# Differential attention: a unit's first steps moved in front of the logits in the first and in the last head

## The chip, the core and the metric

One core of a Trainium2 chip runs the whole program. The time is that of the device in microseconds (us), from the start to the end of one execution; the runs of the kernel before have a median of 1680.06 us (three runs, 1678.5 to 1680.33).

## What is computed

The reference is one step of a backbone with two layers: a gated linear attention layer and a differential attention layer, each followed by a SwiGLU FFN, over 512 sample tokens and 128 prompt tokens, width 1024, all in float32. The change touches the differential attention only. Cut to what matters (q and k of the sample tokens are rotated by `apply_rope` first; the prompt tokens attend among themselves; the 512 sample tokens attend to 256 old keys and to each other):

```python
q, k, v = diff_qkv(h, w_qkv)                     # 8 heads; q, k: 2 maps of 64; v: 128
s = jnp.einsum('bqhcd,bkhcd->bhcqk', qi, k) * (DIFF_DH ** -0.5)
p = jax.nn.softmax(s, axis=-1)
w = p[:, :, 0] - lam * p[:, :, 1]
o = jnp.einsum('bhqk,bkhv->bqhv', w, v)
o = rmsnorm(o, g_head) * (1.0 - lam_init)
x = x + gate * (o.reshape(B, T, 1024) @ w_out)
```

## The kernel before, in words

Every engine has its own instruction stream, written out by hand, and they meet at semaphores only. TensorE takes its matmuls in the order of the text.

**Units.** A unit is the product of a 1024x128 block of weights with the normed activations of all 640 tokens: 8 steps, one for each 128 rows of the weights, of 6 matmuls each (`tile_products`, L826). Float32 precision comes from three products: high weights by high activations, high by low, low by high. So each block is loaded into `w_raw` (SyncE, `load`, L578), its high part is made by ScalarE (`split_hi`, L1522) and its low part by VectorE (`split_lo`, L2280). There are two weight buffers; units take them in turn (slot 0, slot 1). A head has three units, for q, k and v (j = 0, 1, 2); behind the last head the same places are filled by the output projection's units, which have six or seven steps at first (`out_steps`, L1334). All these units but one sum in the same accumulator, `acc[0]`, so the first step of a unit waits until VectorE has read the unit before (`unit_scaled`, L3030, for a head's units; `out_add`, L3178, which adds an output unit to x in three instructions).

**Logits.** For each head there are four tiles of 128 queries, with two maps each, and the prompt's own tile. `logits` (L1399) writes the two maps of a tile into two of three rotating buffers in PSUM (work, side and the second accumulator `acc[1]`), whose order is the list `RING` (L472): tile 0 takes two, the prompt's tile the third, and tile 1 takes the two of tile 0 again. `begin` (L1298) waits until the buffer has been read by its last user. That user is ScalarE's exponential (`exps`, L2092), which itself waits for VectorE's maximum (`maxima`, L3108). VectorE then combines the two maps (`combine`), TensorE turns the result (`w_turn`), ScalarE copies it and TensorE multiplies it with the values.

**Periods.** All engines go through periods p = -1 to 8. In period p TensorE does head p's logits and turns, and between them the steps of head p+1's units, so that each waits for the other as little as may be. The text of TensorE's period is at L1457, ScalarE's at L2184, VectorE's at L3188. In period 8 and in the units behind period 7 the output projection takes the place of the next head. In period 0 head 0's v unit is the last thing before the first logits: VectorE reads its result (`unit_scaled(0, 2)`) behind the low parts of the old and new keys (`past_lo`, `k_lo_part`), the copy of the new key (`k_keep`) and the split of the next unit's weights (`unit_lo(1, 0)`). SyncE's queue carries in turn the rotation copies of q and k (`rotation`, L697) and the loads of the next head's weights (`head_load`, L677; `out_load`, L683); GpSimd's queue carries the old keys and values, and the new ones out.

The wait that the first step of head 1's first unit makes (slot 1, so the last branch):

```python
                    if h == 0:
                        pe.wait_ge(acc_free[0], pair)
                    elif slot == 0:
                        pe.wait_ge(acc_free[1], pair)
                    else:
                        pe.wait_ge(acc_free[0], pair + 1)
```

Of the kernel before, what the change touches and what calls it, by code (L numbers as in the profile page):

```python
# [37 lines left out]
AH, DH = 8, 64  # L38
# [35 lines left out]
def program(nc, x_prompt, x_sample, state_f, state_b, cache_k, cache_v, c, c_ctx, w_ada, b_ada, g_mix, g_ffn,  # L74
# [3 lines left out]
    with ctx:  # L78
# [443 lines left out]
        def live(h):  # L522
            return 0 <= h < AH
# [301 lines left out]
        def _(pe):  # L825
# [485 lines left out]
            def unit_steps(h, j, a, b):  # L1311

                if h >= AH:
                    out_steps(3 * (h - AH) + j, a, b)
                    return
                if not live(h) or (h == 0 and j < 2):
                    return
                pair, slot = head_unit(h, j)
                if a == 0:
                    pe.wait_ge(lo_ready, unit(pair, slot) + 1)  # L1320
# [6 lines that stand above are left out]
                for k in range(a, b):  # L1327
                    mm = tile_products(slot, k, KD, h_hi_k, h_lo_k, acc[0], 2)
                    if k == KD - 1:
                        mm.then_inc(unit_mm, 1)  # L1330
                    elif (h, j) == (AH - 1, 2):
                        mm.then_inc(h_read, 1)
# [66 lines left out]
            def logits(h, q):  # L1399
                if not live(h):  # L1400
                    return
                names = [f"S{q}{m}" for m in range(2)]
                outs = [begin(h, name) for name in names]
                if q == 0:
                    operands_ready(h)
                for a, b in ((0, 512), (512, SK)):
                    map_products(h, [out[:, a:b] for out in outs], slice(q * P, (q + 1) * P), slice(a, b),
                                 names if b == SK else None)
# [20 lines left out]
            def values(h, pp):  # L1429
                if not live(h):  # L1430
                    return
                out = begin(h, f"O{pp}")
                for q in (2 * pp, 2 * pp + 1):
                    pe.wait_ge(buf_free[buf_of(h, f"T{q}")], count_of(h, f"T{q}") + 1)
                if pp == 0:
                    pe.wait_ge(vp_in[h % 2], 16 * (h // 2 + 1))
                    pe.wait_ge(buf_free[buf_of(h, "VT")], count_of(h, "VT") + 1)
                for t in range(SK // P):
                    mm = pe.matmul(out[:, 0:2 * P], vv[h % 2][:, t, :], wt[pp][:, t, :],  # L1439
                                   start=(t == 0), stop=(t == SK // P - 1))  # L1440
                if pp:
                    mm = pe.matmul(out[:, 512:512 + P], vv[h % 2][:, KT - 1, :], wtp[:, :], start=True, stop=True)
                mm.then_inc(buf_mm[buf_of(h, f"O{pp}")], 1)
# [13 lines left out]
            def period(p):  # L1457

                values(p - 1, 1)
                logits(p, 0)  # L1460
                prompt_logits(p)
                unit_steps(p + 1, 0, 0, 4)
                o_squares_sum(p - 1)
                logits(p, 1)
                unit_steps(p + 1, 0, 4, 6)
                v_turn(p)
                unit_steps(p + 1, 0, 6, 8)
                logits(p, 2)
                unit_steps(p + 1, 1, 0, 2)
                w_turn(p, 0)  # L1470
                unit_steps(p + 1, 1, 2, 8)
                logits(p, 3)
                unit_steps(p + 1, 2, 0, 2)
                if p < 0:
                    k_turn(0)
                w_turn(p, 1)
                unit_steps(p + 1, 2, 2, 5)
                w_turn(p, 2)
                unit_steps(p + 1, 2, 5, 8)
                w_turn(p, 3)  # L1480
                if p >= 0:
                    k_turn(p + 1)
                values(p, 0)
# [37 lines left out]
        def _(act):  # L1521
# [603 lines left out]
            def w_read(h, q):  # L2125
                if not live(h):
                    return
                out = done(h, f"T{q}")
                op = act.activation(wt[q // 2][:, :, (q % 2) * P:(q % 2 + 1) * P],
                                    out[:, 0:SK].rearrange("p (t n) -> p t n", n=P), ACT.Copy)  # L2130
                if q:
                    free(op, h, f"T{q}")
# [51 lines left out]
            def period(p):  # L2184

                past_hi(p)
                w_read(p - 1, 3)
                k_hi_part(p)
                if p == 0:
                    unit_hi(1, 0)  # L2190
                    unit_read(0, 2)
                o_read(p - 1, 0)
                last_o_hi(p, KD - 2)
                unit_hi(p + 1, 1)
                last_o_hi(p, 2, 3)
                o_read(p - 1, 1)
                o_square(p - 1)
                exps(p, 0, 0)
                exps(p, 0, 1)
                prompt_exps(p)  # L2200
                scaled(p, 0)
                last_o_hi(p, 4, 5)
                o_log(p - 1)
                exps(p, 1, 1)
                exps(p, 1, 0)
                scaled(p, 4)
                unit_read(p + 1, 0)
                v_copy(p)
                o_exp(p - 1)
                unit_hi(p + 1, 2)  # L2210
                last_o_hi(p, KD - 1)
                w_read(p, 0)
                exps(p, 2, 1)
                exps(p, 2, 0)
                scaled(p, 1)
                unit_read(p + 1, 1)
                prompt_w_read(p)
                scaled(p, 2)
                exps(p, 3, 1)
                exps(p, 3, 0)  # L2220
                scaled(p, 3)
                w_read(p, 1)
                w_read(p, 2)
                q_hi_part(p + 1)
                if p >= 0:
                    unit_hi(p + 2, 0)
                    last_o_hi(p, 0, 1)
                    unit_read(p + 1, 2)
# [50 lines left out]
        def _(dve):  # L2279
# [908 lines left out]
            def period(p):  # L3188

                past_lo(p)  # L3190
                k_lo_part(p)
                k_keep(p)
                unit_lo(p + 1, 0)
                if p == 0:
                    unit_scaled(0, 2)
                last_o_lo(p, 2, 3, KD - 2)
                if p == AH:
                    for name in ("T13", "T2", "T4"):
                        weight_sum(1, 0, name)
                maxima(p, 0, 0)  # L3200
                maxima(p, 0, 1)
                o_square_lo(p - 1)
                prompt_maxima(p)
                norms(p, 0)
                last_o_lo(p, 4, 5)
                o_variance(p - 1)
                maxima(p, 1, 1)
                maxima(p, 1, 0)
                norms(p, 4)
                combine(p, 0)  # L3210
                unit_lo(p + 1, 1)
                if p >= 0:
                    unit_scaled(p + 1, 0)
                combine(p, 4)
                norms(p, 1)
                out_add(p, 0)
                maxima(p, 2, 0)
                maxima(p, 2, 1)
                out_add(p, 3)
                o_newton(p - 1)  # L3220
                if p == AH:
                    o_scale(p - 1)
                unit_lo(p + 1, 2)
                out_add(p, 4)
                last_o_lo(p, KD - 1)
                if p == AH:
                    split_lo(*out_unit(6), OUT_KT[6])
                out_add(p, 5)
                norms(p, 2)
                combine(p, 1)  # L3230
                unit_scaled(p + 1, 1)
                out_add(p, 1)
                maxima(p, 3, 1)
                maxima(p, 3, 0)
                combine(p, 2)
                rope_sin(p + 1, 0)
                rope_cos(p + 1, 0)
                norms(p, 3)
                rope_add(p + 1, 0)
                rope_cos(p + 1, 1)  # L3240
                combine(p, 3)
                rope_sin(p + 1, 1)
                if p < AH:
                    o_scale(p - 1)
                q_lo_part(p + 1)
                rope_add(p + 1, 1)
                out_add(p, 2)
                if p >= 0:
                    unit_scaled(p + 1, 2)
                last_o_lo(p, 0, 1)  # L3250
# [106 lines left out]
```

## Time and profile before

| | |
|---|---|
| median of 3 runs | 1680.06 us |
| profiled execution, in all | 1682.3 us |
| its span | 1680.5 us |
| TensorE busy (matmuls) | 1621.0 us, 96% |
| VectorE, ScalarE, GpSimd busy | 1174.0, 845.0, 97.4 us |
| chain that ended last | TensorE 92%, VectorE 3%, ScalarE 2% |
| granted TensorE clock, mean | 0.985 |

The profile is one execution; its span is what the engines' records cover, and the time in all is a little longer. The attention periods lie at about 865 to 1163 us of the span, some 37 us for each head. A row of the time order has the start, the duration, the engine, the line of the kernel, the operation, what is written from what, and how many such instructions stand together; in brackets, the idle time of the engine before it and the instruction that ended it. Durations overlap a little, since the next instruction starts before the last one is written back. The granted clock is a share of full speed.

### The profile page before, as it was taken

The numbers are of one execution on the slowest core, as the hardware profiler recorded it, in microseconds if no ns is written. First come the engines' busy times: TensorE is split into PE (matmuls) and PEld (weight loads), VectorE is DVE, ScalarE is ACT, GpSimd is POOL, SyncE is SP. The second block draws the span as 40 slices with busy tenths as digits, with TensorE's granted clock in tenths as the row PEclk, the third lists the DMA queues.
The fourth block names the chain that finished last, engine by engine and source line by source line (L and its number), as shares of the span: only waits on it lengthen the run. The fifth ranks groups of instructions, "written<-read, shape, count | busy, mean of one in ns | idle before, by whom it ended". The sixth has DMA issues, their size and how long they took to land.

```text
span 1680.5 us, 28352 instructions
## 1 busy us (share of the span) xinstructions
PE 1621.0 (96%) x10988; PEld 1521.9 (91%) x10988; DVE 1174.0 (70%) x2033; ACT 845.0 (50%) x1460; POOL 97.4 (6%) x147
## 2 busy tenths in 40 slices
PE   6999999998999999999999999999889999999997
PEld 4878788798999999999989999998879999999997
DVE  5536455678857858767767887787878588586775
ACT  4534525356524515334547777786655244253444
POOL 1111110200000000000000000000000000000000
PEclk9999999999999999999999999999989999999998
DMA  9544453632333323432322222213122232232312
GB/s 319 167 154 138 134 186 107 198 85 76 120 107 101 120 70 88 122 92 91 100 72 75 65 74 63 78 45 120 56 76 70 79 88 80 67 97 64 101 40 87
DMA packets 230393, 171.06 MB, mean 102 GB/s; under 512 B 10643, under 2 KB 210998, under 8 KB 230262
## 3 DMA queue, kind: packets, MB, share of 16 engines
q1 hardware_dynamic: 216182, 120.37, 24.8%
q0 software_dynamic: 14080, 48.90, 8.5%
q8 instruction: 88, 1.44, 0.3%
q14 instruction: 43, 0.35, 0.1%
HBM read 160.32 MB, written 4.72 MB: 98 GB/s over the span
## 4 chain that ended last, share of the span: by engine, by line
PE 92%; DVE 3%; ACT 2%; issue 1%; DMA 1%; SPq 0%; POOL 0%; DVEq 0%; ACTq 0%; POOLq 0%
PE acc L832 44%; PE acc L1215 28%; PE side L1215 4%; PE side L1394 2%; PE side L1439 1%; PE acc L1439 1%; PE side L867 1%; PE work L1368 1%; DVE x L2658 1%; PE work L867 1%; PE side L1054 1%; PE acc L1036 0%; PE acc L867 0%; PE work L1394 0%; PE acc L1088 0%
## 5 line engine op out<-in xcount | busy, mean ns | idle before, releaser
L832 PE MATMUL acc<-h_hi,w_hi 128*128 128x320 f32 x1006 | 243.9, 324 | 8.5 <-DVE w_lo L2283 2.5
L832 PE MATMUL acc<-h_lo,w_hi 128*128 128x320 f32 x1006 | 231.8, 312 | 0.0
L832 PE MATMUL acc<-h_hi,w_lo 128*128 128x320 f32 x1006 | 230.8, 311 | 0.0
L832 PEld LDWEIGHTS acc<-h_hi,w_hi 128*128 128x128 f32 x1006 | 166.3, 191 | 35.7 <-issue 21.0
L2658 DVE SCALAR_TENSOR_TENSOR x<-acc,mods,x 128x320 f32<-128x320 f32 (+2 forms) x249 | 94.1, 434 | 135.2 <-PE acc L832 135.1
L1215 PE MATMUL acc<-h_hi,w_hi 128*128 128x322 f32 x616 | 169.9, 317 | 13.6 <-ACT u_t L1924 13.6
L832 PEld LDWEIGHTS acc<-h_lo,w_hi 128*128 128x128 f32 x1006 | 170.9, 191 | 0.0
L832 PEld LDWEIGHTS acc<-h_hi,w_lo 128*128 128x128 f32 x1006 | 170.8, 190 | 0.0
L1215 PE MATMUL acc<-ax_hi,ff_hi 128*128 128x322 f32 x528 | 166.9, 316 | 3.5 <-issue 3.5
L1215 PE MATMUL acc<-ax_lo,ff_hi 128*128 128x322 f32 x528 | 165.5, 313 | 0.0
L1215 PE MATMUL acc<-ax_hi,ff_lo 128*128 128x322 f32 x528 | 165.5, 313 | 0.0
L832 PE MATMUL acc<-hid_hi,ff_hi 128*128 128x320 f32 x616 | 140.7, 310 | 0.0
L832 PE MATMUL acc<-hid_lo,ff_hi 128*128 128x320 f32 x616 | 140.3, 309 | 0.0
L832 PE MATMUL acc<-hid_hi,ff_lo 128*128 128x320 f32 x616 | 140.3, 309 | 0.0
L1215 PE MATMUL acc<-h_lo,w_hi 128*128 128x322 f32 x440 | 138.7, 315 | 0.0
L2283 DVE TENSOR_TENSOR w_lo<-w_raw,w_hi 128x1024 fp32r<-128x1024 f32 (+2 forms) x66 | 78.4, 1189 | 74.0 <-ACT w_hi L1527 73.8
L1215 PEld LDWEIGHTS acc<-h_hi,w_hi 128*128 128x128 f32 x616 | 112.8, 193 | 14.6 <-issue 14.0
L1215 PE MATMUL acc<-h_hi,w_lo 128*128 128x322 f32 x440 | 121.2, 310 | 0.0
L1215 PEld LDWEIGHTS acc<-ax_hi,ff_hi 128*128 128x128 f32 x528 | 101.3, 192 | 8.1 <-issue 7.9
L832 PEld LDWEIGHTS acc<-hid_lo,ff_hi 128*128 128x128 f32 x616 | 103.0, 188 | 0.0
L832 PEld LDWEIGHTS acc<-hid_hi,ff_lo 128*128 128x128 f32 x616 | 103.0, 188 | 0.0
L832 PEld LDWEIGHTS acc<-hid_hi,ff_hi 128*128 128x128 f32 x616 | 102.8, 188 | 0.0
(461 smaller groups left out, 3569.8 us busy)
## 6 DMA issues: line engine op xcount, KB each, us to landing
a_raw<-in_w_ada_dram POOLq DMA_DIRECT2D x80, 512.0 KB, 6.0
ff_raw<-in_w_ffn_gate_dram SPq DMA_DIRECT2D x88, 256.0 KB, 3.3
ff_raw<-in_w_ffn_up_dram SPq DMA_DIRECT2D x88, 256.0 KB, 4.3
w_raw<-in_w_gla_in_dram SPq DMA_DIRECT2D x24, 512.0 KB, 3.8
ff_raw<-in_w_ffn_down_dram SPq DMA_DIRECT2D x32, 384.0 KB, 3.4
w_raw<-in_w_diff_qkv_dram SPq DMA_DIRECT2D x24, 512.0 KB, 3.9
ff_raw<-in_w_ffn_down_dram SPq DMA_DIRECT2D x32, 320.0 KB, 3.2
a_left<-in_w_ada_dram SPq DMA_DIRECT2D x8, 512.0 KB, 9.7
```

The lines of the kernel that those rows point to most:

```text
L832: mm = pe.matmul(out[:, s, 0:HALF + s * more], w[:, k * P:(k + 1) * P], a(k)[:, s * HALF:(s + 1) * HALF + s * more], start=(k == 0 and n = ...
L867: mm = pe.matmul(out[q * CG:(q + 1) * CG, 0:512], cond_at(2 * q + j, place), a_raw[q][:, j, :], start=(b == lo and j == 0), stop=(b == hi ...
L1054: mm = pe.matmul(out[cc * CH:(cc + 1) * CH, r], q_d[d][:, t * P + cc * CH:t * P + (cc + 1) * CH], state_in(d, 2 * t + cc), start=False, st ...
L1215: mm = pe.matmul(out, w[:, j * P:(j + 1) * P], x_part, start=(name in ("P1", "P7", "P2") and j == 0 and n == 0), stop=(j == JT - 1 and n = ...
L1368: mm = pe.transpose(out[:, t * P:(t + 1) * P], tile, ident[:, :])
L1394: mm = pe.matmul(outs[m], qq[h % 2][rows, cols], kk[h % 2][rows, keys], start=(n == 0), stop=(n == 2))
L1439: mm = pe.matmul(out[:, 0:2 * P], vv[h % 2][:, t, :], wt[pp][:, t, :], start=(t == 0), stop=(t == SK // P - 1))
L2283: dve.tensor_tensor(w_lo[slot][:, 0:kt * P], w_raw[slot][:, 0:kt * P], w_hi[slot][:, 0:kt * P].bitcast(F32), ALU.subtract).then_inc(lo_rea ...
L2658: op = dve.scalar_tensor_tensor(out=xk[:, lo:hi], in0=src[:, half, lo - half * HALF:hi - half * HALF], scalar=mods[:, one, v], in1=xk[:, l ...
```

## The change

Nothing is computed differently; instructions change places.

In the first head (p = 0) TensorE does the first four steps of head 1's first unit before the logits of tile 0 instead of behind them and the prompt's. Its weights' high part is made by ScalarE before the new key's high part instead of after it, and its low part by VectorE in the period before (p = -1), between the cosine product of the key and `combine` (which does nothing there). In the last head (p = 7) TensorE does the first three steps of the second output unit before the logits of tile 2 instead of two steps behind them. VectorE makes that unit's low weights before `o_variance`, and adds the first output unit to x (`out_add(p, 0)`) between the two maxima of tile 1 instead of behind the norms of tile 1; `out_add(p, 0)` does something in period 7 only.

```diff
@@ TensorE's period
                 values(p - 1, 1)
+                if p == 0:
+                    unit_steps(1, 0, 0, 4)
                 logits(p, 0)
                 prompt_logits(p)
-                unit_steps(p + 1, 0, 0, 4)
+                if p:
+                    unit_steps(p + 1, 0, 0, 4)
                 o_squares_sum(p - 1)
                 logits(p, 1)
                 unit_steps(p + 1, 0, 4, 6)
                 v_turn(p)
                 unit_steps(p + 1, 0, 6, 8)
+                if p == AH - 1:
+                    unit_steps(p + 1, 1, 0, 3)
                 logits(p, 2)
-                unit_steps(p + 1, 1, 0, 2)
+                if p != AH - 1:
+                    unit_steps(p + 1, 1, 0, 2)
                 w_turn(p, 0)
-                unit_steps(p + 1, 1, 2, 8)
+                unit_steps(p + 1, 1, 3 if p == AH - 1 else 2, 8)
@@ ScalarE's period
                 w_read(p - 1, 3)
+                if p == 0:
+                    unit_hi(1, 0)
                 k_hi_part(p)
                 if p == 0:
-                    unit_hi(1, 0)
                     unit_read(0, 2)
@@ VectorE's period
                 k_keep(p)
-                unit_lo(p + 1, 0)
+                if p:
+                    unit_lo(p + 1, 0)
                 if p == 0:
                     unit_scaled(0, 2)
...
                 last_o_lo(p, 4, 5)
+                if p == AH - 1:
+                    unit_lo(p + 1, 1)
                 o_variance(p - 1)
                 maxima(p, 1, 1)
+                out_add(p, 0)
                 maxima(p, 1, 0)
                 norms(p, 4)
                 combine(p, 0)
-                unit_lo(p + 1, 1)
+                if p != AH - 1:
+                    unit_lo(p + 1, 1)
...
                 norms(p, 1)
-                out_add(p, 0)
...
                 rope_cos(p + 1, 1)
+                if p == -1:
+                    unit_lo(1, 0)
                 combine(p, 3)
```

## Rows read from the trace of the kernel before

**Rows 1.** The page, its first part: busy time and share of the span of each engine.

```profile
PE 1621.0 (96%) x10988; PEld 1521.9 (91%) x10988; DVE 1174.0 (70%) x2033; ACT 845.0 (50%) x1460; POOL 97.4 (6%) x147
```

**Rows 2.** TensorE's waits, whole span: who ended them, us, times, longest.

```profile
PE side L1394 <- ACT w_map L2103: 2.9, 1, 2.9
```

**Rows 3.** Time order of TensorE, first head: logits, four steps, logits of tile 1.

```profile
864.82 0.47 PE L1394 MATMUL side<-kk_hi,q_hi 64*128 64x512 f32 x1 [2.50 <-DVE kk_lo L3089]
...
866.86 0.87 PE L832 MATMUL acc<-h_hi,w_hi 128*128 128x320 f32 x2 [0.42 <-DVE v_f L3047]
...
871.85 0.50 PE L1394 MATMUL side<-kk_hi,q_hi 64*128 64x512 f32 x1
```

**Rows 4.** Time order of VectorE, first head: rotated key, split, read of v.

```profile
860.90 0.69 DVE L3069 TENSOR_TENSOR rotated<-rotated,sin_t 128x512 f32<-128x512 f32 x1 [3.02 <-DMA rotated<-k_f]
...
864.68 1.23 DVE L2283 TENSOR_TENSOR w_lo<-w_raw,w_hi 128x1024 fp32r<-128x1024 f32 x1
...
865.89 0.82 DVE L3047 TENSOR_TENSOR v_f<-acc,rstd_a 128x640 f32<-128x640 f32 x1
```

**Rows 5.** First head: ScalarE's idle time, the weights' load, such loads' time to landing.

```profile
862.97 0.74 ACT L2090 ACTIVATE kk_hi<-k_f 128x640 fp32r<-128x640 f32 x1 [4.64 <-DVE k_f L3075]
...
853.53 0.58 SPq L578 DMA_DIRECT2D w_raw<-in_w_diff_qkv_dram  x1
...
w_raw<-in_w_diff_qkv_dram SPq DMA_DIRECT2D x3, 512.0 KB, 4.0
```

**Rows 6.** Last head, tile 0: logits (TensorE), first maximum (VectorE), last exponential's sum (ScalarE).

```profile
1125.44 0.49 PE L1394 MATMUL side<-kk_hi,q_hi 64*128 64x512 f32 x1
...
1126.80 0.96 DVE L3112 TENSOR_REDUCE stat<-work 128x1 f32<-128x768 f32 x1 [0.46 <-PE work L1394]
...
1129.47 0.19 ACT L2103 ACTIVATION_READ_ACCUMULATOR p<-side,stat 128x1 f32 x1
```

**Rows 7.** Stretches of TensorE: length, busy time (instructions), granted clock, DMA share, GB/s.

```profile
866.86:869.67 2.81, 2.81 (x10) 0.50 0.79 231
1139.46:1146.29 6.83, 6.22 (x28) 0.51 0.99 304
1126.97:1130.60 3.63, 3.63 (x27) 1.00 0.24 71
```

**Rows 8.** The same, around stalls of 1.59 us (to 337.38) and 2.21 us (to 1193.11).

```profile
335.79:340.80 5.01, 3.42 (x23) 1.00 0.71 204
1190.90:1197.40 6.50, 4.29 (x19) 0.74 0.00 0
```

**Rows 9.** Time order of TensorE, last head: tile 2's logits, two steps, turn, third unit.

```profile
1138.32 0.50 PE L1394 MATMUL side<-kk_hi,q_hi 64*128 64x512 f32 x1 [2.87 <-ACT w_map L2103]
...
1140.36 0.87 PE L832 MATMUL acc<-h_hi,w_hi 128*128 128x320 f32 x2 [0.61 <-issue]
...
1143.70 1.49 PE L1368 MATMUL work<-ident,w_map 128*128 128x128 f32 x6
...
1151.04 0.54 PE L832 MATMUL acc<-h_hi,w_hi 128*128 128x320 f32 x2 [0.48 <-issue]
```

**Rows 10.** Time order of VectorE, last head: from the variance to the second unit's x update.

```profile
1133.49 0.82 DVE L3153 TENSOR_SCALAR o_var<-work 128x640 f32<-128x640 f32 x1
...
1140.18 0.95 DVE L3112 TENSOR_REDUCE stat<-side 128x1 f32<-128x768 f32 x1
...
1144.36 0.95 DVE L2283 TENSOR_TENSOR w_lo<-w_raw,w_hi 128x768 fp32r<-128x768 f32 x1
1148.04 0.17 DVE L3127 RECIPROCAL stat<-stat 128x2 f32<-128x2 f32 x1 [2.74 <-ACT w_map L2103]
...
1148.87 1.02 DVE L3140 SCALAR_TENSOR_TENSOR w_map<-p,stat,w_map 128x768 f32<-128x768 f32 x1 [0.47 <-ACT w_map L2123]
1149.81 1.13 DVE L2658 SCALAR_TENSOR_TENSOR x<-acc,mods,x 128x320 f32<-128x320 f32 x3
```

**Rows 11.** Time order of ScalarE, last head: the copy of tile 0's turned weights.

```profile
1145.43 0.81 ACT L2129 ACTIVATE wt<-work 128x768 f32<-128x768 f32 x1 [4.93 <-PE work L1368]
```

## The prediction, made before the changed kernel ran

> **What bounds the kernel now.** I read the page first, then TensorE's waits, then the time order of TensorE, VectorE and ScalarE around the two edited places. TensorE is busy for 96% of the 1680.5 us [rows 1], so only what it waits for, and the clock it is granted, can give time. Its longest wait in the attention stage is 2.9 us for an exponential, in the last head [rows 2]; in front of the first head's logits it waits 2.50 us for the low part of the new keys. With the short waits beside them (0.42, 0.61 and 0.48 us [rows 3, 9]) they are 6.9 us: nothing here can bring much more than that and the low clock behind it.
>
> In the first head TensorE ends v's unit at 862.32 (864.82 less 2.50), runs the logits of tile 0 and of the prompt until 866.44 (866.86 less 0.42), and then waits for VectorE's read of v's accumulator. Four steps of head 1's first unit start at 866.86, the logits of tile 1 follow at 871.85 without a wait [rows 3]. In the last head it ends the transposes of v at 1135.45 (1138.32 less 2.87), the logits of tile 2 at 1139.75, and starts the second output unit at 1140.36 and the third at 1151.04 [rows 9].
>
> **The clock.** TensorE has half clock, the lower of 1.2 and 2.4 GHz, in 866.86 to 869.67, after 2.50 us of idling, and in 1139.46 to 1146.29, after 2.87 and 0.61 us [rows 7]. Four steps take 3.63 us at full clock [rows 7] and 4.99 in the first head with the low stretch in them (866.86 to 871.85 [rows 3]): such a stretch costs 1.4 us. Two steps wholly at low clock take 3.34 us (1140.36 to 1143.70 [rows 9]), so four take 6.7. Elsewhere a stall of 1.59 us left the granted clock at full, and one that ended at 1193.11 after 2.21 us was followed by low clock [rows 8]. Between those two lengths I can only bound.
>
> **First head.** The four steps (24 matmuls, 24 weight loads) move ahead of 18 logits matmuls, and their weights must be split earlier. That is easy: the load was issued at 853.53 and such loads land after 4.0 us, about 857.6, while ScalarE idles 4.64 us until 862.97 and VectorE 3.02 us until 860.90 [rows 4, 5]. Two splits, each at most the 1.23 us of VectorE's row [rows 4], end by 860.7 even if ScalarE begins at 858.3, just ahead of VectorE's turn at 860.90. I cost them at nothing; a load 0.5 us later would delay the key's chain by 0.3. SyncE's next load into that buffer waits for this split and goes out 5 us earlier; its weights are wanted in the middle of the head, so that gains nothing. GpSimd's queue is not touched.
>
> But the steps write the accumulator that holds v's result, so they wait until VectorE has read it, and that read stays behind the key's low part and the copy of the new key. It ends now at 865.89 + 0.82 = 866.71. Without the split in front (1.23 us, 1.15 by the distance of the starts) it ends at 865.56, and TensorE starts the steps 0.15 later, as now: **865.71**. The idle of 2.50 us before the logits becomes one of 3.39 before the steps. The logits' operands are ready at 864.8, but TensorE takes its matmuls in order. With one low stretch as now the steps take 4.99 us: logits of tile 0 at **870.70** instead of 864.82.
>
> Next late are the logits of tile 1. They write the two buffers of tile 0's logits, which come free with tile 0's two exponentials. Where that runs undisturbed, in the last head, the logits start at 1125.44, the first maximum at 1126.80, and the last exponential's sum is read by 1129.66 [rows 6]: 4.22 us, 4.27 to the next matmul. Today the four steps cover this. After the change only the prompt's logits stand there (1.62 us with tile 0's, 864.82 to 866.44), so TensorE stalls 2.65 us and starts tile 1 at 870.70 + 4.27 = **874.97**, against 871.85: **3.1 us later**. From there to the last head TensorE has no wait, so it reaches the end in full. Bounds: steps at full clock (3.63) give +1.8, wholly at low clock (6.7) +4.8. The second stall, longer than the 2.21 us that was followed by low clock, brings a second low stretch: +1.4, with ends 0 and 1.6. First head: **+4.5**, from +1.8 to +6.4.
>
> **Last head.** Three steps of the second output unit go ahead of tile 2's logits. They need its low weights, and the first output unit read from the accumulator; both are moved up. VectorE's variance started at 1133.49; the split (0.95) now stands before it, so variance, first maximum of tile 1 and x update follow at about 1134.4, 1135.1 and 1135.95 (the first output unit is done before v's transposes, in time). The update takes 1.13 us [rows 10]: 1137.1. The steps start at **1137.2**: 1.75 us of idling instead of 2.87. The second maximum is late by 1.9 us and its exponential ends at about 1139.0 (0.95 for each by half of the 1.90 between 1127.76 and 1129.66 [rows 6]); the logarithm, 0.9 later through the variance, is in time for that. The steps' 2.7 us (three quarters of 3.63) last until 1139.9 and cover it.
>
> Logits of tile 2 then run 1139.95 to 1141.4, against 1139.75 now. What decides the third unit's start is VectorE's chain behind them: two maxima and three Newton instructions (1140.18 to 1144.36), a split (0.95), the norms, the combination (1.02), and the x update of the second unit (1.13) [rows 10]. Today it stands still from 1145.3 to 1148.04, because ScalarE waits for TensorE's turn of tile 0 until 1145.43 [rows 11]. After the change that turn runs at 1141.4 and the chain is unbroken: 1141.35 + 4.18 + 0.95 + 0.2 + 1.02 + 1.13 = 1148.8 (0.2 estimated for the two small norms from the 0.17 of one). Third unit at **1148.9** instead of 1151.04: **-2.1 us**, with a new stall of 2.5 us before it, as TensorE ends tile 3's logits at 1146.4. Output units 3 and 4 are loaded from 1134.4 and 1146.4 on and wanted ten us later: hidden. Clock: the 1.75 us stall is nearer the 1.59 that cost nothing; the 2.5 us one is of the kind that does: +1.4, ends 0 and +2.8. Last head: **-0.7**, from -2.1 to +0.7.
>
> **Sum:** 4.5 - 0.7 = +3.8 us. The profiled execution took 1682.3 us, 2.2 over the median of the three runs, 1680.06; the difference is applied to the median: 1683.9, rounded to **1684.0**.
>
> **A rule on the clock.** The Trainium skill, "TensorE: Matmul & The Clock Gate" (Terms), puts the penalty of throttled time at half of it. By that the stretch of 6.83 us cost 3.4, of which 0.6 was idle anyway, and each 2.8 us stretch 1.4, as the rows have it: the sum by the rule is the same within 0.3. Its section "HAM oscillation" speaks against the change: a kernel that stalls between bursts is throttled again at each burst. The trace agrees for stalls from 2.21 us up, not for the one of 1.59 [rows 8].
>
> **Rivals.** (1) *Every stall costs a low stretch*, that of 1.75 us too, and the low clock lasts through the first steps: +1.4 or +1.7, together 1685.3 to 1687. For it: the low stretch of the last head lasts 6.83 us though only 3.5 were idle [rows 7, 9]. Against: the stall of 1.59. Chance 0.18; this is the case of the skill's rule on bursts. (2) *The clock holds* behind the second stall of the first head and the 2.5 us stall of the last: 1683.9 - 2.8 = 1681.1, or 1679.8 with the first steps at full clock. For it: a fall depends on the moment of the stall as well; against: 2.21 us was enough. Chance 0.24. (3) *Faster: the accumulator is free early.* Could the steps start behind v's unit at 862.5, they would end at 866.1 at full clock, tile 1 would start at 870.4, 1.5 us earlier, and with the last head's -2.1 the time is 1676.5. It decides as soon as v's read ends before about 863. Against: today's 0.42 us wait is on that very read [rows 3], and its place behind the key stays. Chance 0.08.
>
> **How the numbers follow.** The forecast has 0.50. A measurement of this kernel can tell 0.2%, 3.4 us, from no change, so the border, 1683.4, lies inside the forecast's own spread (1682.4 to 1685.6): I give it 0.35 slower and 0.15 same. With rival 1 slower is 0.53, with rival 2 same is 0.39, and rival 3 is faster, 0.08. The range, 1679.8 to 1687.5, takes in rivals 1 and 2 and leaves out rival 3 and chains of ends.
>
> **What would show it.** In the changed profile: one wait of TensorE of about 3.4 us on v_f ahead of the first steps, none on kk_lo, and one of about 2.6 us on an exponential before tile 1's logits, with low clock behind both. In the last head a wait of 1.75 us on the x update before the steps, none before tile 2's logits, and 2.5 us on the x update before the third unit. I am wrong if tile 1's logits in the first head start without a wait, or if VectorE reads v before the key's low part.

## The result and the profile after

The changed kernel takes 1686.24 us (median of 7 runs, 1683.34 to 1687.58) against 1679.52 us for the kernel before (7 runs, 1678.02 to 1680.87). The ratio is 1.0035, with a 95% interval of 1.0024 to 1.0045: by it the change costs 5.9 us (4.0 to 7.6); the two medians alone differ by 6.7. The prediction was 1684.0, 3.8 us slower, with a range of 1679.8 to 1687.5: the measured time is in the range, but above the spread that the forecast itself had (1682.4 to 1685.6).

TensorE's three longest entries in the list of its waits in the attention stage of the changed kernel (who waited for whom, us in total, times, longest) answer to [rows 2, 3, 9]:

```profile
PE acc L832 <- issue: 3.5, 2, 2.4
PE acc L832 <- DVE v_f L3054: 3.3, 1, 3.3
PE side L1394 <- ACT p L2109: 2.8, 1, 2.8
```

The two long waits of before, on the low part of the keys and on the exponential in the last head, are gone. Three others of 3.3, 2.8 and 2.4 us stand in their place. "issue" means that no record names who ended the wait; the time order of VectorE below lets one infer it.

The first head in TensorE's time order of the changed kernel: the first of the four steps, then the logits of tiles 0, 1 and 2.

```profile
865.68 0.53 PE L832 MATMUL acc<-h_hi,w_hi 128*128 128x320 f32 x2 [3.33 <-DVE v_f L3054]
...
870.92 0.50 PE L1394 MATMUL side<-kk_hi,q_hi 64*128 64x512 f32 x1
...
875.29 0.47 PE L1394 MATMUL side<-kk_hi,q_hi 64*128 64x512 f32 x1 [2.75 <-ACT p L2109]
...
882.37 0.50 PE L1394 MATMUL side<-kk_hi,q_hi 64*128 64x512 f32 x1
```

VectorE there: the read of v's result, then idle for 6.74 us until tile 0's logits are there.

```profile
863.71 0.82 DVE L3096 TENSOR_TENSOR kk_lo<-k_f,kk_hi 128x640 fp32r<-128x640 f32 x1 [0.47 <-ACT kk_hi L2096]
864.46 0.28 DVE L3113 COPY k_new<-work 128x128 f32<-128x128 f32 x1
...
864.72 0.81 DVE L3054 TENSOR_TENSOR v_f<-acc,rstd_a 128x640 f32<-128x640 f32 x1
872.28 0.96 DVE L3119 TENSOR_REDUCE stat<-side 128x1 f32<-128x768 f32 x1 [6.74 <-PE side L1394]
```

Stretches of TensorE in the changed kernel (length, busy time, granted clock, DMA share, GB/s): the four steps, from tile 1's logits to tile 2's, and the third output unit's first steps.

```profile
865.68:870.92 5.24, 5.24 (x24) 0.67 0.11 38
875.29:882.37 7.08, 7.08 (x42) 0.76 0.00 1
1153.81:1157.01 3.20, 3.20 (x13) 0.53 0.51 145
```

The reader should see three starts. The steps start at 865.68, the predicted 865.71. Tile 1's logits start at 875.29 (predicted 874.97) instead of 871.85 [rows 3], 3.4 us later. From there to tile 2's logits is 7.08 us, where it was 5.52 us; the difference of 1.56 us goes with the second low stretch (granted clock 0.76).

The last head in TensorE's time order of the changed kernel: the transposes of v, the second unit's first steps, the logits of tiles 2 and 3, the third unit.

```profile
1140.26 0.74 PE L1368 MATMUL work<-ident,v_f 128*128 128x128 f32 x5 [0.42 <-DVE o_var L3160]
...
1142.12 0.53 PE L832 MATMUL acc<-h_hi,w_hi 128*128 128x320 f32 x2 [1.12 <-issue]
...
1144.94 0.50 PE L1394 MATMUL side<-kk_hi,q_hi 64*128 64x512 f32 x1
...
1150.09 0.49 PE L1394 MATMUL side<-kk_hi,q_hi 64*128 64x512 f32 x1 [0.28 <-ACT w_map L2109]
...
1153.81 0.87 PE L832 MATMUL acc<-h_hi,w_hi 128*128 128x320 f32 x2 [2.42 <-issue]
```

VectorE in front of the second unit's steps: the x update of the first output unit, which ends at 1142.01, just before the steps start at 1142.12.

```profile
1140.89 1.12 DVE L2665 SCALAR_TENSOR_TENSOR x<-acc,mods,x 128x320 f32<-128x320 f32 x3
```

And VectorE behind tile 2's logits: the chain from the first maximum over the Newton step to the x update that frees the accumulator, unbroken (each row's start is the end of the one before, less the overlap). It ends at 1153.71, and the third unit starts at 1153.81. It answers to [rows 10], where VectorE stood still until 1148.04.

```profile
1146.30 0.96 DVE L3119 TENSOR_REDUCE stat<-side 128x1 f32<-128x768 f32 x1 [1.29 <-PE side L1394]
1147.18 0.95 DVE L3119 TENSOR_REDUCE stat<-acc 128x1 f32<-128x768 f32 x1
1148.04 0.81 DVE L2318 SCALAR_TENSOR_TENSOR o_sqr<-o_inv 128x640 f32<-128x640 f32 x1
1148.89 0.83 DVE L2321 TENSOR_TENSOR o_sqr<-o_sqr,o_var 128x640 f32<-128x640 f32 x1
1149.75 0.82 DVE L2323 SCALAR_TENSOR_TENSOR o_inv<-o_sqr,o_inv 128x640 f32<-128x640 f32 x1
1150.49 0.95 DVE L2290 TENSOR_TENSOR w_lo<-w_raw,w_hi 128x768 fp32r<-128x768 f32 x1
1151.36 0.16 DVE L3134 RECIPROCAL stat<-stat 128x2 f32<-128x2 f32 x1
1151.56 0.16 DVE L3138 TENSOR_TENSOR stat<-stat,lam_neg 128x1 f32<-128x1 f32 x1
1151.64 1.02 DVE L3147 SCALAR_TENSOR_TENSOR w_map<-p,stat,w_map 128x768 f32<-128x768 f32 x1
1152.58 1.13 DVE L2665 SCALAR_TENSOR_TENSOR x<-acc,mods,x 128x320 f32<-128x320 f32 x3
```

### The profile page after: what moved, and what is told of

Read it like the earlier page. It is cut to its first block, busy times and chain, and to the rows that moved or that the text cites. A ratio compares the mean times of both kernels' runs of the same rounds, so it can differ in the third digit from the quotient of the medians.

```text
span 1684.4 us, 28352 instructions
## 1 busy us (share of the span) xinstructions
PE 1620.9 (96%) x10988; PEld 1522.5 (90%) x10988; DVE 1174.0 (70%) x2033; ACT 845.3 (50%) x1460; POOL 97.4 (6%) x147
## 4 chain that ended last, share of the span: by engine, by line
PE 92%; DVE 4%; ACT 2%; issue 1%; DMA 0%; SPq 0%; POOL 0%; DVEq 0%; ACTq 0%; POOLq 0%
PE acc L832 44%; PE acc L1215 28%; PE side L1215 4%; PE side L1394 2%; PE side L1439 1%; PE acc L1439 1%; PE side L867 1%; PE work L1368 1%; DVE x L2665 1%; PE work L867 1%; PE side L1054 1%; PE acc L1036 0%; PE work L1394 0%; PE acc L867 0%; PE acc L1088 0%
```

## The experiments

Each was timed beside the kernel before; gains and losses in us are the ratio's distance from 1 times 1680, and an interval of 0.001 each way is 1.7 us. The table gives the ratios and two distances in each one's profile, worked out from the starts in TensorE's time order. "First head" is from the first head's key transposes to tile 0's logits of the last head; "last head" from those logits to the third output unit's first matmul. The first distance takes in six more heads, which no edit touches. Each distance is from one execution, so differences of some tenths of a us between rows mean little.

| kernel | ratio to before (95%) | first head, us | last head, us |
|---|---|---|---|
| before, first profile | 1 | 268.98 | 25.60 |
| before, profiled again (before_again) | 1.0000 (0.9991 to 1.0009) | 268.95 | 23.95 |
| the change | 1.0035 (1.0024 to 1.0045) | 273.90 | 23.43 |
| first head's part only (first_only) | 1.0030 (1.0020 to 1.0039) | 273.83 | 25.33 |
| last head's part only (last_only) | 1.0004 (0.9996 to 1.0013) | 269.26 | 23.41 |
| steps spread (cover) | 1.0007 (0.9998 to 1.0016) | 270.84 | 24.84 |
| v read first (vread) | 1.0008 (0.9999 to 1.0017) | 270.75 | 24.88 |
| both of these (both) | 0.9994 (0.9985 to 1.0003) | 267.41 | 25.43 |
| early split only (split_only) | 0.9999 (0.9990 to 1.0008) | 269.42 | 25.59 |
| late Newton step (late_newton) | 0.9976 (0.9966 to 0.9986) | 269.25 | 20.94 |
| late Newton step, no steps moved (newton_only) | 0.9995 (0.9986 to 1.0004) | 269.23 | 23.36 |
| both, with late Newton step (best) | 0.9977 (0.9967 to 0.9987) | 269.17 | 20.92 |
| late Newton step and early split (best2) | 0.9977 (0.9968 to 0.9986) | 268.95 | 20.90 |

### The kernel before, profiled again

No edit.

> The kernel before, unchanged, profiled once more and timed. It serves to see what of the first profile was chance. The first profiled execution took 1682.3 us, 2.2 over the median, and had 6.83 us of low clock in the last head. Theory (the clock's fall depends on the moment as well): this profile has the same waits (2.50 and 0.42 us in the first head, 2.87, 0.61 and 0.48 us in the last) within 0.1 us, but stretches of low clock of another length, and its time differs by about 0.45 us for each us of low clock. Rival (the stretches belong to the kernel): the same stretches within 0.5 us.

Measured: ratio 1.0000, this profile at 1679.53 us in all, 2.8 under the first. TensorE's waits in its attention stage:

```profile
PE side L1394 <- ACT w_map L2103: 2.9, 1, 2.9
PE side L1394 <- DVE kk_lo L3089: 2.8, 1, 2.8
PE acc L832 <- issue: 0.9, 1, 0.9
```

The low clock comes at another moment here: the logits behind the long wait run slow from the start (0.79 us a row where the first profile has 0.50 [rows 9]).

```profile
1136.96 0.79 PE L1394 MATMUL side<-kk_hi,q_hi 64*128 64x512 f32 x1 [2.85 <-ACT w_map L2103]
```

The stretch 1130 to 1165, first in the first profile of before, then in this one:

```profile
1130.00:1165.00 35.00, 30.76 (x195) 0.90 0.42 132
```

```profile
1130.00:1165.00 35.00, 30.97 (x205) 0.95 0.41 132
```

The long waits are much alike (2.76 and 2.85 instead of 2.50 and 2.87), the short ones are not: those of 0.42 and 0.61 us are absent, as the slower logits in front of them fill that time, and the last is 0.87 instead of 0.48. So the theory's "within 0.1 us" is missed, and a wait of some tenths says as much of the clock as of the kernel. The low clock differs: 35 us at 0.90 are about 7 us at half clock, at 0.95 half as many, and the third output unit comes 1.65 us earlier (23.95 instead of 25.60). That is not the whole of the 2.8 us between the two executions. Another 1.3 us lies ahead of the attention, where the change does nothing: the first head's key transposes start at 856.46 in the first profile and at 855.13 in this one.

```profile
856.46 0.44 PE L1368 MATMUL work<-ident,k_past 128*128 128x128 f32 x2 [0.28 <-ACT k_f L2061]
```

```profile
855.13 0.44 PE L1368 MATMUL work<-ident,k_past 128*128 128x128 f32 x2 [0.27 <-ACT k_f L2061]
```

So the profile on which I predicted had bad luck in the place where I saw a gain. In the seven kernels and profiles with the last head's order of before on both engines, the distance lies anywhere from 23.95 to 25.60.

### The two halves of the change

The first head's part alone is the change with this taken back:

```diff
-                if p == AH - 1:
-                    unit_steps(p + 1, 1, 0, 3)
                 logits(p, 2)
-                if p != AH - 1:
-                    unit_steps(p + 1, 1, 0, 2)
+                unit_steps(p + 1, 1, 0, 2)
...
-                if p == AH - 1:
-                    unit_lo(p + 1, 1)
                 o_variance(p - 1)
                 maxima(p, 1, 1)
-                out_add(p, 0)
```

The last head's part alone is the change with this taken back:

```diff
-                if p == 0:
-                    unit_steps(1, 0, 0, 4)
                 logits(p, 0)
                 prompt_logits(p)
-                if p:
-                    unit_steps(p + 1, 0, 0, 4)
+                unit_steps(p + 1, 0, 0, 4)
...
-                if p == -1:
-                    unit_lo(1, 0)
```

and in both cases with the other lines that belong to that head.

> Only the first head's part of the change. Theory (v's read in front, cover lost behind): TensorE waits 3.3 us on v_f before the first steps and 2.7 us on the exponential before tile 1's logits; tile 1's logits are 3.4 us later than before, tile 2's 5.0 us with a second low stretch, 3.4 if the clock holds; the ratio to before 1.0020 to 1.0035. Rival (the two heads share the loss): ratio below 1.0015.

> Only the last head's part of the change. Theory: the third output unit starts 2.1 us earlier than before with a wait of 2.4 us in front of it; the time is 0.5 to 2 us shorter, ratio 0.9985 to 1.0000. Rival (the last head's part costs too, by the split in front of the variance and the x update between the maxima): 1 us or more longer, ratio over 1.0006.

Measured: 1.0030 for the first head's part, 1.0004 for the last head's. In the first, TensorE waits 3.36 us on v_f and 2.76 on the exponential, tile 1's logits stand 18.81 us behind the key transposes (before: 15.39, so 3.4 later) and tile 2's 25.85 (20.91, 4.9 later): as expected. The rival, a loss shared between the heads, is out: the first head alone has nearly all of it. In the second, the third unit has its wait of 2.41 us and comes after 23.41 us, 2.2 earlier than in the first profile of before but only 0.5 earlier than in the second; a low stretch follows it. Its ratio lies between the theory's upper bound and the rival's lower one, so the gain of 0.5 to 2 us that I expected did not come, and its interval holds both no change and a loss of 2 us: the last head's part brought no gain that can be measured. An estimate from the rows agrees: 2.2 us less on the first profile or 0.5 on the second, and 1.4 more for the new low stretch, come to -0.8 or +0.9 us.

### Steps spread

```diff
                 if p == 0:
-                    unit_steps(1, 0, 0, 4)
+                    unit_steps(1, 0, 0, 2)
                 logits(p, 0)
                 prompt_logits(p)
-                if p:
-                    unit_steps(p + 1, 0, 0, 4)
+                unit_steps(p + 1, 0, *((0, 4) if p else (2, 5)))
                 o_squares_sum(p - 1)
                 logits(p, 1)
-                unit_steps(p + 1, 0, 4, 6)
+                unit_steps(p + 1, 0, 4 if p else 5, 6)
```

> The first head's part alone, with the steps of head 1's first unit spread: two before tile 0's logits, three between the prompt's logits and tile 1's, three behind tile 1's. Theory (the second stall is lost cover): the wait on the exponential is gone, the wait of 3.3 us on v_f stays; tile 1's logits start 0.5 to 1.5 us later than before instead of 3.4; the time is 2.5 to 4 us below that of first_only. Rival (the second stall belongs to the buffers and the exponential, wherever the steps stand): the wait stays over 1.5 us before tile 1's or tile 2's logits and the time is within 1 us of first_only.

Measured: 1.0007, 3.7 us below the first head's part alone by the medians (1681.46 against 1685.12). TensorE's time order: tile 0's logits, tile 1's without a wait, and a new wait before head 1's second unit:

```profile
864.52 0.87 PE L832 MATMUL acc<-h_hi,w_hi 128*128 128x320 f32 x2 [3.73 <-DVE v_f L3050]
...
867.84 0.50 PE L1394 MATMUL side<-kk_hi,q_hi 64*128 64x512 f32 x1
...
872.20 0.49 PE L1394 MATMUL side<-kk_hi,q_hi 64*128 64x512 f32 x1
...
879.07 0.53 PE L832 MATMUL acc<-h_hi,w_hi 128*128 128x320 f32 x2 [0.90 <-DVE q_f L3050]
```

The wait on the exponential is gone once three steps stand in front of tile 1's logits: the second stall was lost cover. From tile 0's logits to tile 1's is 4.36 us here and 4.37 in the change; in one it is filled, in the other 2.75 of it are idle. Tile 1's logits are 1.9 us later than before, not 0.5 to 1.5, since the wait on v_f came out at 3.73 and the steps ran at low clock (0.87 us for the first row, 0.53 in the change). The 0.90 us on q_f are new: the first unit now ends early, and VectorE reads it where it always did.

### v read first

To the first head's part alone, in VectorE's period:

```diff
+                if p == 0:
+                    unit_scaled(0, 2)
                 past_lo(p)
                 k_lo_part(p)
                 k_keep(p)
                 if p:
                     unit_lo(p + 1, 0)
-                if p == 0:
-                    unit_scaled(0, 2)
```

> The first head's part alone with its four steps ahead, and VectorE reads v's result right behind the key's rope_add, before the keys' low parts. Theory (v's read sets the first stall): TensorE's wait on v_f shrinks from 3.3 to 1.5 us and no low clock follows it; the steps take 3.7 us instead of 5.2; the wait on the exponential before tile 1's logits stays at 2.7 us; the time is 3 us below that of first_only, ratio to before 1.0005 to 1.0018. Rival (the key's low part sets it): the wait stays over 2.5 us, ratio over 1.0025.

Measured: 1.0008 (0.9999 to 1.0017); the interval of the first head's part alone (1.0020 to 1.0039) lies above it. TensorE's time order:

```profile
863.51 0.53 PE L832 MATMUL acc<-h_hi,w_hi 128*128 128x320 f32 x2 [1.81 <-DVE v_f L3051]
...
867.21 0.50 PE L1394 MATMUL side<-kk_hi,q_hi 64*128 64x512 f32 x1
...
871.57 0.47 PE L1394 MATMUL side<-kk_hi,q_hi 64*128 64x512 f32 x1 [2.76 <-ACT p L2106]
```

The wait before the steps falls from 3.36 to 1.81 us (1.5 expected) and the steps take 3.70 us, at full clock: no low stretch follows. The wait on the exponential is untouched. So the first stall was set by the place of v's read in VectorE's order, not by the keys.

### Both

The two diffs above together, on the first head's part alone.

> v's read in front as in vread and the steps spread 2, 3, 3 as in cover; the last head as before. Theory (the two costs add and both can be had back): one wait of 1.5 us on v_f, none of more than 0.3 us before tile 1's logits, no low clock in the first head; tile 1's logits 1.5 to 2 us earlier than before; ratio 0.9983 to 0.9993. Rival (the first head was as good as it can be): ratio 0.9997 or over.

Measured: 0.9994 (0.9985 to 1.0003), between the theory's and the rival's ratios, and the interval holds 1. Time order of TensorE:

```profile
864.00 0.53 PE L832 MATMUL acc<-h_hi,w_hi 128*128 128x320 f32 x2 [1.69 <-DVE v_f L3050]
...
870.29 0.49 PE L1394 MATMUL side<-kk_hi,q_hi 64*128 64x512 f32 x1
```

Tile 1's logits are 1.55 us earlier than before and the whole first head 1.6 us shorter, with no low clock in it (granted clock 1.00 from 856.45 to 900). By the profile the idea of the change pays in the first head once both of its costs are paid for; by the times the gain of 1.0 us can't be told from none.

### Early split only

ScalarE's and VectorE's edits of the first head's part, with TensorE's order of before. Against the first head's part alone:

```diff
-                if p == 0:
-                    unit_steps(1, 0, 0, 4)
                 logits(p, 0)
                 prompt_logits(p)
-                if p:
-                    unit_steps(p + 1, 0, 0, 4)
+                unit_steps(p + 1, 0, 0, 4)
```

> Of the first head's part only the split of head 1's first unit is made early (ScalarE and VectorE); TensorE's order is that of before. Theory (the early split costs nothing and frees VectorE): the wait of 2.5 us (to 3.1) on kk_lo stays, the wait of 0.42 us on v_f is gone, everything behind it is 0.4 us earlier at the same clock; ratio 0.9990 to 1.0003. Rival (the early split is what delays the first head, through the key's chain or the loads): kk_lo's wait grows by over 0.3 us, ratio over 1.0008.

Measured: 0.9999 (0.9990 to 1.0008). The wait on v_f is gone, but it is absent from the second profile of before too, so that shows nothing; the wait on kk_lo is 3.13 us in this profile, against 2.50 and 2.76 in the two of before. That 0.3 to 0.6 us looks like the rival, but kernels whose first head is that of before show 2.93 and 3.09 too, and the early split together with the late Newton step (below) shows 2.77, so it is the spread of this wait. By the ratio the early split doesn't cost the 5 us. Whether it is worth the 0.4 us stays below what can be told.

### Late Newton step

On the last head's part alone, in VectorE's period:

```diff
                 out_add(p, 3)
-                o_newton(p - 1)
+                if p != AH - 1:
+                    o_newton(p - 1)
...
                 out_add(p, 5)
+                out_add(p, 1)
                 norms(p, 2)
                 combine(p, 1)
                 unit_scaled(p + 1, 1)
-                out_add(p, 1)
...
                 rope_sin(p + 1, 1)
+                if p == AH - 1:
+                    o_newton(p - 1)
                 if p < AH:
                     o_scale(p - 1)
```

> The last head's part alone, with VectorE's three Newton instructions moved behind the combination of tile 3 and the second unit's x update in front of the norms of tile 2. Theory (VectorE's chain behind tile 2's logits holds the third unit): the wait of 2.4 us before the third unit falls to 0.3 us or less, no low clock follows, the third unit starts 4 to 4.5 us earlier than in the first profile of before; the time is 2.5 to 3.8 us below that of last_only, ratio to before 0.9975 to 0.9990. Rival (the unit's weights or the buffers hold it): the wait stays over 1.5 us, ratio over 0.9997.

> The kernel before with only the Newton instructions late and the second unit's x update early in the last head; no step moves. Theory (the chain behind tile 2's logits is the bound only once the steps stand in front of them): the wait of 2.9 us before tile 2's logits stays, that of 0.5 to 0.9 us before the third unit goes; ratio 0.9990 to 0.9998. Rival (the reordered VectorE is the whole gain of late_newton): ratio 0.9982 or less.

Measured: 0.9976 with the change's last head (1676.0 us, 4.0 below before and 4.7 below the last head's part alone), 0.9995 without. The third unit of the first of them in TensorE's time order, right behind tile 3's logits and with no wait:

```profile
1144.46 0.50 PE L1394 MATMUL side<-kk_hi,q_hi 64*128 64x512 f32 x1 [0.27 <-ACT w_map L2106]
...
1145.72 0.56 PE L832 MATMUL acc<-h_hi,w_hi 128*128 128x320 f32 x2
```

and the second unit's x update in VectorE's, now waiting for TensorE instead of the other way round:

```profile
1142.41 0.95 DVE L2286 TENSOR_TENSOR w_lo<-w_raw,w_hi 128x768 fp32r<-128x768 f32 x1
1144.22 1.13 DVE L2661 SCALAR_TENSOR_TENSOR x<-acc,mods,x 128x320 f32<-128x320 f32 x3 [0.86 <-PE acc L832]
```

The stretch 1130 to 1165 of this profile has full clock:

```profile
1130.00:1165.00 35.00, 32.89 (x226) 1.00 0.45 132
```

This is the simplest version that beats both kernels. The gain was a little above the 2.5 to 3.8 us expected against the last head's part, inside the two intervals. VectorE's reordering alone isn't it: without the moved steps it gives 0.9995, and without the reordering the moved steps give 1.0004. Each takes away a wait behind which the other's stands. The diff has two parts, the Newton step put later and the x update put earlier; they were not run apart, so which of them counts is not shown.

### Combinations

"Both" (the two diffs of "steps spread" and "v read first") or the early split, each on the change together with the diff of the late Newton step:

> both and late_newton together. Theory (the heads are independent and TensorE has no slack between them): the gains add, ratio 0.996 to 0.998. Rival (something else takes the time back, such as the loads behind the attention): ratio over 0.999.

> late_newton with split_only's early split; in the first head TensorE's order is that of before. Theory: the two gains add, ratio 0.9966 to 0.9980, below late_newton by up to 0.0005. Rival: same as or slower than late_newton, 0.9976 or over, if the 0.42 us are lost again to the clock.

Measured: 0.9977 in both cases, no better than the late Newton step alone. For the first, the ratio is within the 0.996 to 0.998 expected, but nothing was added: in this profile the first wait is 1.87 us and the clock falls right behind it (TensorE's time order, steps and tile 0's logits at 0.79 instead of 0.50 us):

```profile
862.68 0.53 PE L832 MATMUL acc<-h_hi,w_hi 128*128 128x320 f32 x2 [1.87 <-DVE v_f L3053]
...
865.08 0.79 PE L1394 MATMUL side<-kk_hi,q_hi 64*128 64x512 f32 x1
```

Its first head takes 269.17 us where "both" took 267.41. So the first head's gain hangs on whether the clock holds behind that wait. Whether the fall is chance or comes in every execution of this kernel isn't known: it is one profile, and the kernel's nine times lie within 1.1 us. For the second, 0.9977 is in the theory's range and in the rival's, so it decides nothing; a gain of 0.0005 is below what can be told.

## Why the prediction was right, point by point

**First head, the wait ahead of the steps.** Predicted 3.39 us and a start at 865.71; 3.33 and 865.68. That the place of v's read sets it is shown by reading v first, which took 1.55 us off it.

**First head, lost cover.** Predicted a stall of 2.65 us and tile 1's logits 3.1 us late; 2.75 and 3.4, the steps having taken 5.24 instead of 4.99 us. Spreading the steps took the stall away: shown.

**The second low stretch.** Predicted +1.4, measured 7.08 less 5.52, so 1.56. It came in all three profiles with this stall (the change, its first head's part alone, and v read first: 7.08, 7.04 and 7.03 us). The first head as a whole: +4.5 predicted; 4.9 by the profile, 5.0 by the ratio of its half.

**Early splits at no cost.** ScalarE's split ran at 858.25 and VectorE's at 859.33 to 860.56; the rotated key was read at 860.88 as before. Right.

**Last head.** The steps started after a wait of 1.12 us and not 1.75, because the transposes of v waited 0.42 us and ended 0.6 us later than I had put them: they write the buffer that the variance reads, and the variance had been moved behind the split. I had costed only ScalarE's side of that delay. It came to nothing, as the x update set the start of the steps anyway. The third unit's wait was 2.42 us (predicted 2.5), and its start 23.43 us behind the head's first logits, 2.2 us less than in the first profile (predicted 2.1), and a low stretch followed it (predicted).

**Where the sum was off.** Profile against profile the sum was good: the spans are 1684.4 and 1680.5 us, 3.9 us apart where I had 3.8 (4.9 longer in the first head's distance, 1.0 shorter in the rest, where I had 4.5 and 0.7). The times are further apart. The term "-0.7 for the last head" was mis-sized: it measured +0.7 us by its own ratio (-0.7 to +2.2). The step that failed is "the difference is applied to the median". The profiled execution of before stood 2.2 us over the median, and I treated that as lying outside the change. Of the 2.8 us to the second profile of before, 1.3 do lie outside, ahead of the attention, but 1.65 lie in the last head: about 7 us of low clock instead of 3.5. The new low stretch behind the third unit thus replaced a cheaper one than the one I had set it against. With a last head of about 0 the same sum gives 4.5 us, inside the interval of 4.0 to 7.6; what is left to 5.9 is less than the measurement can tell. That 1684.0 and 1686.24 share the range owes something to the range's width: it was drawn to take in rivals 1 and 2.

**Rivals.** The clock held nowhere that I had expected it to fall (rival 2 is out). Rival 1 forecast 1685.3 to 1687, and the time lies there, but not by its mechanism: the first steps ran partly at full clock (granted 0.67), and the stall in front of the last head's steps was 1.12 us, not 1.75, and the clock held behind it. A stall of 1.75 us was thus not put to the test in this kernel. Rival 3 needed v's read to end before 863, 6.5 us behind the first key transposes; the kernels that read v first end it 7.4 to 7.5 us behind them and are the nearest to it: 0.9994 with the steps spread.

The Trainium skill's rule that a kernel which stalls between bursts is throttled again ("TensorE: Matmul & The Clock Gate", HAM oscillation) is borne out by the stalls of 2.4 us and more, each of which has low clock behind it in these profiles, and not by shorter ones: that a stall of 2.21 us is followed by low clock, on which I built, was one case, and it fails in six of the 13 profiles (see the last section). In the first head the added waits are 3.2 us and the added time 4.9.

## What to carry to other kernels

Work that is moved in front of a wait is also taken away from the place it came from: before moving it, ask what it covered there, and count the time from the producer's start until its buffers are free again (here 4.3 us from one tile's logits to the next, of which the moved steps had filled 3.6). Then ask what the moved work itself waits for: an accumulator that has to be read first turned the wait of 2.5 us (up to 3.1 in other profiles) into one of 3.3, and one line in the reading engine's order was worth 1.5 us of it. And where a wait disappears and the time stays, look who is late next: here it was VectorE's chain behind the logits, and putting three of its instructions later and one update earlier turned a change worth nothing in the last head into one worth 4.0 us.

## What was not expected of the hardware

Behind a wait of about 2 us the fall of the granted clock can't be told from the wait. The clearest case lies behind the attention, in code that no edit touches: a wait of 2.21 us on an x update, within 0.01 us the same in all 13 profiles. In seven of them low clock follows, as in the kernel before [rows 8]; in six it does not, as in the first head's part alone. The 5.24 us behind the wait, first in the first profile of before, then in that of the first head's part alone (length, busy time, instructions, granted clock, DMA share, GB/s):

```profile
1193.11:1198.35 5.24, 5.24 (x25) 0.67 0.00 0
```

```profile
1196.71:1201.95 5.24, 5.24 (x40) 1.00 0.00 0
```

These are different kernels. That one and the same kernel differs from execution to execution is shown for the length of the stretch: about 7 us of low clock in the last head of before in one profile and 3.5 in the next. Of the eight profiles with the wait of 2.9 us there, four have the long stretch and four the short one. Waits of 1.59 us (the kernel before), 1.69 ("both") and 1.81 us ("v read first") were not followed by a fall, and one of 1.87 us ("both" with the late Newton step) was; each of the last three is a single profile. A single profile of a kernel with such waits says its time to some 2 us only (the two of before took 1682.3 and 1679.5), more than the whole last head's part was about.
